# Expert stage: remainders formed in place, units with wide rows, two transfers per unit

## The reference, cut to what matters

```python
def expert_block(args):
    xe, e = args                                   # 128 token slots x 1024
    return (jax.nn.silu(xe @ w1[e]) * (xe @ w3[e])) @ w2[e]
# w1, w3: (8, 1024, 2816), w2: (8, 2816, 1024), float32
y = jnp.zeros((n_tok, D), jnp.float32).at[slot_tok].add(yb.astype(jnp.float32) * slot_w[:, None])
```

## Time and profile before

| what | us |
|---|---|
| median of 3 runs | 3139.25 (3137.63 to 3141.74) |
| the profiled execution: its own time | 3138.09 |
| the profiled execution: span | 3136.4 |
| first unit of the first expert starts on PE | 2261.8 |
| last unit of the last expert ends on PE | 3109.4 |

### The profile page before, as it was taken

How to read it: one execution, slowest core, us unless ns; L and a number is a source line. 1 busy time by engine, 2 the same in 40 slices (tenths; PEclk the granted TensorE clock), 3 DMA queues, 4 the chain that set the end, 5 groups by cost and what they waited for, 6 DMA issues and landing times. The chain is left out here.

```text
span 3136.4 us, 35052 instructions
## 1 busy us (share of the span) xinstructions
PE 2739.4 (87%) x12871; PEld 2178.0 (69%) x12871; DVE 1451.2 (46%) x1832; ACT 1285.7 (41%) x1532; POOL 1511.7 (48%) x600
## 2 busy tenths in 40 slices
PE   4987999899888699996868898979599999999997
PEld 2774778687557588875665676747587777777775
DVE  2386312431422323202364324331477787778776
ACT  2421332331332333312421523333366676667765
POOL 0330344143123344433321643606198888879986
PEclk6988999999999899998888999989699999999999
DMA  6236233132112133321235532504399999989996
GB/s 193 81 121 202 81 89 93 34 89 86 41 41 81 42 95 99 99 81 55 71 104 163 146 94 81 146 15 121 122 339 316 320 338 331 324 312 335 347 311 241
DMA packets 271658, 492.34 MB, mean 157 GB/s; under 512 B 14576, under 2 KB 102928, under 8 KB 271376
## 3 DMA queue, kind: packets, MB, share of 16 engines
q1 hardware_dynamic: 271288, 490.18, 47.8%
q10 hardware_dynamic: 216, 0.07, 0.0%
HBM read 489.16 MB, written 1.05 MB: 156 GB/s over the span
## 5 line engine op out<-in xcount | busy, mean ns | idle before, releaser
L279 POOL TENSOR_TENSOR unit_lo<-raw_units,unit_hi 128x1024 fp32r<-128x1024 f32 x248 | 592.5, 2410 | 1123.3 <-ACT unit_hi L271 1123.3
L2114 POOL TENSOR_TENSOR moe_unit_lo<-moe_raw,moe_unit_hi 128x640 fp32r<-128x640 f32 x266 | 739.8, 2808 | 162.4 <-ACT moe_unit_hi L2109 162.2
L2114 DVE TENSOR_TENSOR moe_unit_lo<-moe_raw,moe_unit_hi 128x1408 fp32r<-128x1408 f32 x266 | 541.5, 2044 | 180.4 <-ACT moe_unit_hi L2109 179.0
L2109 ACT ACTIVATE moe_unit_hi<-moe_raw 128x2048 fp32r<-128x2048 f32 x266 | 510.1, 1919 | 275.7 <-PE bank L300 268.8
L271 ACT ACTIVATE unit_hi<-raw_units 128x1024 fp32r<-128x1024 f32 (+1 forms) x250 | 247.6, 1039 | 750.4 <-PE bank L300 584.5
L298 PE MATMUL bank<-unit_hi,hT_hi 128*128 128x512 f32 x880 | 352.0, 400 | 41.0 <-POOL unit_lo L279 13.6
L299 PE MATMUL bank<-unit_lo,hT_hi 128*128 128x512 f32 x880 | 348.1, 396 | 0.0
L300 PE MATMUL bank<-unit_hi,hT_lo 128*128 128x512 f32 x880 | 347.9, 395 | 0.0
L298 PE MATMUL bank<-moe_unit_hi,xe_T_hi 128*128 128x512 f32 (+1 forms) x768 | 297.0, 387 | 12.0 <-DVE moe_unit_lo L2114 8.5
L300 PE MATMUL bank<-moe_unit_hi,xe_T_lo 128*128 128x512 f32 (+1 forms) x768 | 289.5, 377 | 0.0
L299 PE MATMUL bank<-moe_unit_lo,xe_T_hi 128*128 128x512 f32 (+1 forms) x768 | 288.9, 376 | 0.0
(11 more groups left out here) (370 smaller groups left out, 4445.5 us busy)
## 6 DMA issues: line engine op xcount, KB each, us to landing
moe_raw<-in_moe_w SPq DMA_DIRECT2D x270, 1024.0 KB, 5.2
raw_units<-in_w_in SPq DMA_DIRECT2D x160, 512.0 KB, 3.8
ada_unit<-in_ada_w SPq DMA_DIRECT2D x40, 1024.0 KB, 5.3
raw_units<-in_ffn_w SPq DMA_DIRECT2D x66, 512.0 KB, 3.7
raw_units<-in_w_branch SPq DMA_DIRECT2D x48, 512.0 KB, 3.7
ada_first<-in_ada_w SPq DMA_DIRECT2D x8, 1024.0 KB, 12.0
raw_units<-in_w_out SPq DMA_DIRECT2D x16, 512.0 KB, 3.7
constants<-in_consts SPq DMA_DIRECT2D x1, 1124.0 KB, 5.2
```

Of the source, the lines that this page charges most:

```text
L279: eng.tensor_tensor(lo, whole, hi.bitcast(F32), ALU.subtract).then_inc(lo_ready, 1)
L2109: act.activation(moe_hi[:, v % RING, :], moe_raw[:, raw_slot(x, v), :], ACT.Copy).then_inc(hi_m, 1)
L2114: eng.tensor_tensor(moe_lo[:, s, a:b], moe_raw[:, raw_slot(x, v), a:b], moe_hi[:, s, a:b].bitcast(F32), ALU.subtract).then_inc(done, 1)
```

## The change

1. **In place.** `moe_lo` lies on the same 8 slots (`SLOTS`) as `moe_raw`: the remainder overwrites the weights that it came from. The slot is free only when PE has used the unit. The ring of `moe_hi` has 4 buffers, and AHEAD is 3. Six units (`EARLY`) are fetched ahead of the stage.
2. **Remainders on DVE alone.** `lo` covers the whole unit on DVE. POOL does no `lo`; it builds the next expert's `pick` instead, which DVE did.
3. **Wide rows.** Blocks of 1024, 1024 and 768 columns (`WIDE`) take the place of 512 and 256. A unit has two row groups: U = 35, of which 24 are up units (the 8 of the last block are of 0.75 MB) and 11 down units. A wide block has one pair of banks for h1 and one for h3.
4. **Two transfers per unit.** Each carries one row group (4 KB or 3 KB for a partition). SP issues the first, ACT the second, in its iteration ahead of `hi`.
5. **The turn.** `moe_prod` is a whole wide block, two DVE instructions. The turn is in quads of four transposes: `turn_after[q]` is h3_end+1 for the first quad and h3_end+2 for the second.
6. **The expert's end.** ACT writes `moe_ye_hi` straight from the banks by halves, DVE takes `moe_ye_lo` by halves with one instruction each.
7. **The loop** is over passes, with all 8 experts in its body.

```diff
-        RAW_RING, RING, AHEAD = 6, 3, 2
+        SLOTS, RING, AHEAD, EARLY = 8, 4, 3, 6
...
+        moe_lo = at("moe_unit_lo", [P, SLOTS, 2048], F32R, R0)
...
-        NB = 6
+        WIDE = [1024, 1024, 768]
+        NB, NG = len(WIDE), 6
         plan = []
-        for _b in range(NB - 1):
-            plan += [(w, 4 * half, 4, _b * 512, 512) for w in (w1, w3) for half in range(2)]
-        plan += [(w, 0, KD, (NB - 1) * 512, 256) for w in (w1, w3)]
+        for _b, _w in enumerate(WIDE):
+            plan += [(w, 2 * pair, 2, _b * 1024, _w) for w in (w1, w3) for pair in range(KD // 2)]
...
+            for half in halves:
+                sp.dma_start(unit_part(moe_raw, slot, v)[:, half:half + 1, :], src[:, half:half + 1, :]).then_inc(raw_m[slot], 16)
...
-            h1_end = [4 * b + 1 for b in range(NB - 1)] + [up - 2]
-            h3_end = [4 * b + 3 for b in range(NB - 1)] + [up - 1]
-            turn_after = [h1_end[b + 1] for b in range(NB - 2)] + [up - 1, up + 1]
+            h1_end = [8 * b + 3 for b in range(NB)]
+            h3_end = [8 * b + 7 for b in range(NB)]
+            turn_after = [h3_end[q // 2] + 1 + q % 2 for q in range(NG)]
...
+            def lo(dve, i, x, v):
+                at_unit = U * x + v
+                dve.wait_ge(hi_m, NE * U * i + at_unit + 1)
+                n = cols_in(v)
+                dve.tensor_tensor(moe_lo[:, at_unit % SLOTS, 0:n], moe_raw[:, at_unit % SLOTS, 0:n],
+                                  moe_hi[:, at_unit % RING, 0:n].bitcast(F32), ALU.subtract).then_inc(lo_m, 1)
...
                             for u in range(U):
                                 act.wait_ge(used, U * n + u + 1)
+                                if u:
+                                    load_moe(act, x, u - 1 + SLOTS, (1,))
                                 hi(act, i, x, u + AHEAD)
...
+                            for half in range(2):
+                                act.activation(ye[0][:, half * 512:(half + 1) * 512], ps[6 + half][:, :], ACT.Copy,
+                                               scale=w_slot[:, 0:1]).then_inc(ye_out, 1)
...
                                     if u == h3_end[b] + 1:
-                                        dve.wait_ge(silu_out, NB * n + b + 3)
+                                        dve.wait_ge(silu_out, NB * n + b + 2)
                                         dve.wait_ge(used, U * n + h3_end[b] + 2)
+                                        for j in range(2):
+                                            w = min(512, WIDE[b] - 512 * j)
+                                            ins = dve.tensor_tensor(prod[:, 512 * j:512 * j + w], silu[:, 512 * j:512 * j + w],
+                                                                    ps[2 + j][:, 0:w], ALU.mult)
+                                        ins.then_inc(g_done, 1)
...
+                                for q in range(NG):
+                                    if u == turn_after[q]:
...
+                                        pe.wait_ge(g_done, NB * n + q // 2 + 2)
```

More of the change, by code:

```diff
@@ L1926, in program @@
         U = len(plan)
-        assert U % RING == 0 and 2 * U % RAW_RING == 0
-        raw_m = [sem(f"moe_raw_loaded{i}") for i in range(RAW_RING)]
+        assert NE * U % RING == 0 and NE * U % SLOTS == 0
+        raw_m = [sem(f"moe_raw_loaded{i}") for i in range(SLOTS)]
         def unit_part(buf, slot, v):
@@ L1962, in _ @@
                     sp.dma_start(wr[:, :, :], t["moe_router"][0].rearrange("(k p) n -> p k n", p=P)).then_inc(router_in, 16)
-                    for v in range(RAW_RING):
-                        load_moe(sp, 0, 0, v)
+                    for v in range(EARLY):
+                        load_moe(sp, 0, v)
                     sp.wait_ge(router_in, 16)
@@ L2101, in part @@
[L2101 to L2105, removed]
-            def hi(act, i, x, v):
[L2108 to L2130, removed]
-                for j in range(2):
[L2133 to L2136, removed]
+             combined, added, slot_free, pick_turn) = (stage_sem(s) for s in names)
@@ new lines, in moe_experts, with cols_in @@
+            column = at("pick_column", [P, 2, 2], F32, m + 20480)
+            def cols_in(v):
+                _, _, a, _, b = plan[v % U]
+                return a * b
+            def hi(act, i, x, v):
+                at_unit = U * x + v
+                act.wait_ge(raw_m[at_unit % SLOTS], 32 * (NE * U // SLOTS) * i + 32 * (at_unit // SLOTS + 1))
+                n = cols_in(v)
+                act.activation(moe_hi[:, at_unit % RING, 0:n], moe_raw[:, at_unit % SLOTS, 0:n], ACT.Copy).then_inc(hi_m, 1)
@@ L2174, in _ @@
                     passes = sp.value_load(n_pass[0:1, 0:1], min_val=1, max_val=2)
[L2175 to L2181, removed]
+                    for v in range(EARLY, SLOTS):
+                        load_moe(sp, 0, v)
+                    with sp.Fori(0, passes) as i:
+                        for x in range(NE):
+                            for v in range(SLOTS, U + SLOTS):
+                                sp.wait_ge(used, sp.snap(NE * U * i + (U * x + v - SLOTS + 2)))
                                 sp.sem_inc(slot_free, 1)
-                                load_moe(sp, experts[x + v // U], x, v)
-                    for s in range(RAW_RING):
-                        sp.wait_ge(raw_m[s], passes * (NE // 2 * (2 * U // RAW_RING) * 16) + 16)
+                                load_moe(sp, x, v, (0,))
+                    for s in range(SLOTS):
+                        sp.wait_ge(raw_m[s], passes * (NE * U // SLOTS * 32) + 32)
                         sp.sem_inc(slot_free, 1)
@@ L2190, in _ @@
                     passes = pool.value_load(n_pass[0:1, 0:1], min_val=1, max_val=2)
[L2191 to L2196, removed]
+                    build_pick(pool, 0)
+                    with pool.Fori(0, passes) as i:
+                        for x in range(NE):
+                            n = NE * i + x
+                            pool.wait_ge(put_sum, n + 1)
+                            pool.sem_inc(pick_turn, 1)
+                            build_pick(pool, n + 1)
                 @block.scalar
@@ L2203, in copy @@
                         return act.activation(out, in_, ACT.Copy)
[L2205 to L2206 removed]
+                    act.sem_inc(silu_out, 1)
+                    act.sem_inc(ye_out, 2)
                     for v in range(AHEAD):
@@ L2296, in _ @@
                         gather(pe, 0, p)
-                    with pe.Fori(0, passes * (NE // 2)) as i:
-                        for x in range(2):
-                            n = 2 * i + x
+                    with pe.Fori(0, passes) as i:
+                        for x in range(NE):
+                            n = NE * i + x
                             pe.wait_ge(xe_act, 2 * n + 2)
```

153 lines of the change are left out of this document (80 added, 73 removed).

## The result

| | before | after |
|---|---|---|
| median, us (4 runs of each side by side) | 3140.11 | 3222.01 (3214.86 to 3224.14) |
| profiled execution: its own time | 3138.09 | 3222.10 |
| its span | 3136.4 | 3220.6 |
| an expert: third combine piece to the next one's, mean of seven | 106.0 | 116.2 |

The ratio is 1.0258, with an interval of 1.024 to 1.0275: 82 us slower. The forecast was 3241 us, with a range of 3188 to 3275 us.

The account below looks back on a forecast made before the run. PE was taken to set the pace, so its stalls are paid in full: 3138.1 + 77 (turns) + 38 (clock) - 23 (waits gone) + 4 + 6 (heads) = 3240 us, as a median 3241 us, range 3188 to 3275 us.

Parts of the forecast that it names:

- turns: Expert stage: PE stands 3.4, 3.0 and 3.2 us at an expert's three first quads, waiting for DVE's product; +77 us.
- slow clock, turns and heads, less what goes: Half clock after PE's stalls: +38 us behind 24 turns, +6 at heads, less 4.8 for three old spells.
- waits for remainders, gathers, picks: Expert stage: PE's waits for remainders and `moe_ye_lo` go, as AHEAD 3 gives three units of lead; -18 us.
- third piece at the heads: Expert heads: PE's third combine piece waits for DVE's first addition, 2.9 us against 2.4 before; +4 us.
- gaps under 0.3 us: PE's small waits in the stage: taken as unchanged, 0; their going was allowed for in a bound of -34 us.
- Rival 3: Expert stage: transfers lead and PE's stalls only use up time spent waiting for data; no change, 3139 us; chance 0.07.
- Rival 2: DVE's remainder of 2048 columns costs 2.99 us also without POOL; 3268 us; chance 0.14.
- Rival 1: The clock stays up behind the turns, so no slow spells; 3197 us; chance 0.16.
- What goes: Expert stage: PE's waits for remainders and `moe_ye_lo`, and three slow spells behind them, vanish; -23 us, bounds 0 and -34.

Follow-up runs that it names:

- e1: The kernel after with each quad's turn one unit later, and the second gather one unit later as well: 3138.63 us, ratio 1.0004.
- e4: The kernel before with its turns one unit earlier, behind h3_end+1, nothing else of the change: 3235.27 us, ratio 1.0306.
- e3: The kernel after with thirteen result-less matmuls of 512 columns on PE ahead of the wait at each first quad: 3193.58 us, ratio 1.0172.
- e2: The kernel after with the product ahead of the remainder in DVE's iteration: 3135.53 us, ratio 0.9997.
- e8: The kernel after with turns one unit later and POOL taking the last 5/16 of each remainder in place, picks in POOL's iteration 5: 3193.32 us, ratio 1.0178.

## Why the prediction was right, term by term

To compare term by term, every interval between the starts of two matmuls in seven experts was taken, less the pace of its shape (0.2265 us for 512 columns, 0.12 for 256, 0.11 for 128), and put down to what stands at it. Times eight:

| term | predicted, us | measured, us | an expert, before and after |
|---|---|---|---|
| turns | +77 | +82.5 | 0.02, 10.33 |
| slow clock, turns and heads, less what goes | +38 +6 -4.8 | +29.7 | 0.70, 4.41 |
| waits for remainders, gathers, picks | -18 | -23.3 | 2.91, 0 |
| third piece at the heads | +4 | +4.7 | 1.42, 2.01 |
| gaps under 0.3 us | 0 | -11.8 | 2.47, 0.99 |
| sum | +102 | +82 | 106.0, 116.2 |

**The turns** came as worked out, engine by engine. The list of parts held: 0.36 us for ACT's issue (0.38 taken), 1.92 for the rounding, 2.29 for the remainder (2.28), 1.28 for the two products, 6.12 us for the chain (6.03). Only the last seam was off: the transposes start 0.13 to 0.24 us after the product in nearly all turns, where 0.05 was taken. The 24 idle times sum to 78.3 us; the table has 4 us more, because an interval between starts counts also the overlap that a stop costs. That moving the turn by one unit gives all of it back (e1) and that the same move does the same to the kernel before (e4) shows the cause: the order, with a longer chain in front of the product. That the wider units, the ring or the transfers slow the kernel in another way than by this chain is ruled out by e1, which keeps them all. Rival 3 fell with it, since the transfers' rate went down where PE stood.

**Remainder without POOL.** Rival 2 had 2.99 us for it and fell: 2.29 us over 212 of them.

**The clock** is the term that was mis-sized. It was taken behind every turn, 24 times 1.6 us. The price was right, about 1.6 us a spell (e3). The number was not: of 24 idle times of 3.0 to 3.6 us 16 were followed by a spell, one of these of double length, where in the mixer all twelve had been. Length alone does not decide it: the same 3.4 us at the first block were followed by a spell in six experts and not in the third and the sixth. What does decide stays open. Of the heads 6 of 8 were followed, half of them was taken. Rival 1, no slow clock, fell with e3.

**The heads.** 1.85 us at the third piece instead of 2.9. Two parts of that chain were wrong: ACT was not 0.7 us late from the expert's end, and only the first of the two additions is waited for, whose result was there before the pair's end. PE lost 2.01 us there for an expert, against 1.42 before. The working had 2.9 against 2.4, since it added up the waits of PE's weight loads (PEld) for the kernel before. Both figures were about 1 us too high, so that their difference, the forecast +4 us, came out right by luck.

**What goes.** The waits taken as gone did go, with the gather's (0.45 us) and the pick's (0.26 us) on top. The small gaps were set to zero and gave 12 us; the range had them in its bound of -34 us. They shrink in e1 and e2 to the same 1.0 us, so they belong to the new layout, with three units of lead or with longer units. Which of the two wasn't tried.

So the mechanism was right, and turns, waits and heads within 6 us each. The forecast was 19 us above the measured 3222. By the table it is 20 us: the clock (9.5), the small gaps (11.8) and the waits (5.3), less what the turns and the heads cost more (6.2). The errors partly cancel.

## What to carry to other kernels

Where an in-order engine makes something for the engine that sets the pace, a distance in units says nothing until the chain is written out: all that stands ahead of the result in the maker's program, the previous iteration too, against the time of the units between. Giving the maker more columns of each unit, or adding one issue, makes that chain longer and leaves the distance as it is; here three places in the order turned +2.6% into -1.7%. In each iteration, put first what the pace setter waits for soonest.

## What the runs showed of the hardware

- A wait of PE of 3.0 to 3.6 us costs more than itself: in two cases of three it was followed by half clock, which cost about 1.6 us. Thirteen matmuls without use in its place, at 24 places, were worth 28 us in this kernel (e3), 24 of them by the clock.
- ACT's issue of a transfer went out during its own table load:

```profile
2284.18 1.28 ACT L2221 ACT_TABLE_LOAD   x1
2284.99 0.36 ACTq L1940 DMA_DIRECT2D moe_raw<-in_moe_w  x1
2285.47 1.09 ACT L2221 ACTIVATE moe_silu<-bank 128x512 f32<-128x512 f32 x2
```

The load runs from 2284.18 to 2285.46, the issue from 2284.99 to 2285.35. An issue isn't always in ACT's chain.
- A copy of 128x4 on POOL took 1.58 us beside DVE's remainder, at all eight experts (e8), and 0.19 us in the kernel after, where DVE was idle at that moment. The time of such a small piece on POOL depends on what DVE does.
